# Products of cached keys and sample queries: from VectorE to GpSimd, a page per instruction

## What is computed

```python
q, k, v, u = _project(xs, pos_s, ...)                      # 8 sample rows: RMSNorm, x @ w_in, rotary
k_past = cache_k[l][page_table].reshape(bs, n_past, DIFF_HEADS, 2, QK_DIM)
v_past = cache_v[l][page_table].reshape(bs, n_past, DIFF_HEADS, V_DIM)

def _diff_attn_sample(q, k_new, v_new, k_past, v_past, lam):
    s = jnp.concatenate([_scores(q, k_past), ...], axis=-1)    # einsum over 64 columns, 4 heads x 2 components
    a = _diff_weights(s, lam)                                  # softmax of component 0 minus lam * component 1
    o_past = jnp.einsum('bhqk,bkhd->bqhd', a[..., :n_past], v_past)
    ...
```

## Time and profile before

| | us |
|---|---|
| median of 3 runs | 1735.47 |
| lowest, highest | 1733.54, 1738.26 |
| span of the profiled execution | 1736.7 |
| VectorE busy | 781.7 |
| GpSimd busy | 96.3 |
| 128 key products on VectorE, busy | 157.7 |
| 128 key sums on VectorE, busy | 156.2 |

### The profile page before, as it was taken

How to read it: one execution, slowest core, us unless ns; L and a number is a source line. 1 busy time by engine, 2 the same in 40 slices (tenths; PEclk the granted TensorE clock), 3 DMA queues, 4 the chain that set the end, 5 groups by cost and what they waited for, 6 DMA issues and landing times.

```text
span 1736.7 us, 32091 instructions
## 1 busy us (share of the span) xinstructions
PE 1476.6 (85%) x11950; PEld 593.4 (34%) x11951; DVE 781.7 (45%) x1158; ACT 356.2 (21%) x822; POOL 96.3 (6%) x173
## 2 busy tenths in 40 slices
PE   3868887779788978999999899898899999898870
PEld 2433333346433353333333333232233332232220
DVE  2689879997786335112322232132132132131316
ACT  3212212232222111111211212112112122121220
POOL 0000010000000000000100000000000000000000
PEclk8989995689898857999999999899899999999985
DMA  9557888989898685579999999999999999999976
GB/s 328 179 187 261 279 292 268 335 286 304 297 297 274 241 359 205 226 320 403 428 419 417 418 405 414 401 406 409 395 411 410 403 429 412 395 428 428 426 327 252
DMA packets 127292, 598.10 MB, mean 344 GB/s; under 512 B 20503, under 2 KB 20517, under 8 KB 102026
## 3 DMA queue, kind: packets, MB, share of 16 engines
q1 hardware_dynamic: 109088, 560.20, 81.7%
q10 hardware_dynamic: 8634, 20.00, 3.4%
q0 software_dynamic: 9504, 17.06, 2.6%
HBM read 589.36 MB, written 25.87 MB: 354 GB/s over the span
## 4 chain that ended last, share of the span: by engine, by line
PE 40%; DMA 19%; DVE 2%; issue 1%; ACT 0%; DVEq 0%; SPq 0%; ACTq 0%
PE bank L1511 25%; DMA wts<-in_w_gate_up 19%; PE bank L1548 7%; PE bank L1530 4%; PE bank L1501 1%; PE bank L1618 1%; DVE v_ring L2137 1%; PE bank L1559 1%; PE bank L1599 0%; DVE q_b L2137 0%; DMA h_tok<-h_rows,v_tok 0%; ACT k_T L1155 0%; DVEq L2125 0%; ACT k_T L1138 0%; DVEq L2126 0%
## 5 line engine op out<-in xcount | busy, mean ns | idle before, releaser
L1511 PE MATMUL bank<-wts,h_T 128*32 128x512 f32 x4032 | 447.9, 600 | 17.3 <-DMA wts<-in_w_gate_up 17.3
L2059 DVE TENSOR_SCALAR q_T<-bank 128x512 f32<-128x512 f32 x32 | 22.1, 692 | 640.4 <-PE bank L1511 640.4
L1511 PEld LDWEIGHTS bank<-wts,h_T 128*32 128x32 f32 x4032 | 128.7, 111 | 320.6 <-issue 292.0
L1548 PE MATMUL bank<-wts,k_T 128*32 128x512 f32 x2048 | 229.0, 599 | 7.3 <-issue 4.9
L1530 PE MATMUL bank<-wts,h_T 128*32 128x512 f32 x992 | 129.5, 663 | 47.2 <-DMA wts<-in_w_gate_up 45.4
L1658 DVE TENSOR_TENSOR wts<-wts,q_b 128x1024 f32<-128x1024 f32 x128 | 157.7, 1232 | 23.0 <-DMA wts<-in_cache_k 17.3
L1661 DVE TENSOR_REDUCE sc<-wts 128x16 f32<-128x1024 f32 x128 | 156.2, 1220 | 4.4
L1145 ACT ACTIVATE h_T<-bank 128x512 f32<-128x512 f32 x66 | 35.9, 595 | 576.4 <-PE bank L1501 576.4
L1548 PEld LDWEIGHTS bank<-wts,k_T 128*32 128x32 f32 x2048 | 65.0, 111 | 148.8 <-issue 139.4
L1223 PE MATMUL bank<-wts,h_T 128*8 128x128 f32 (+1 forms) x480 | 93.3, 472 | 11.9 <-ACT h_T L854 6.4
L1155 ACT ACTIVATE k_T<-bank 32x256 f32<-32x256 f32 x256 | 95.7, 374 | 14.2 <-PE bank L1548 10.9
(11 more groups left out here) (328 smaller groups left out, 1372.5 us busy)
## 6 DMA issues: line engine op xcount, KB each, us to landing
wts<-in_w_gate_up SPq DMA_DIRECT2D x126, 2048.0 KB, 18.4
wts<-in_w_down SPq DMA_DIRECT2D x64, 2048.0 KB, 26.6
wts<-in_cache_k SPq DMA_DIRECT2D x256, 256.0 KB, 3.7
v_ring<-in_cache_v SPq DMA_DIRECT2D x160, 256.0 KB, 3.8
wts<-in_cache_v SPq DMA_DIRECT2D x96, 256.0 KB, 3.9
wts<-in_w_in SPq DMA_DIRECT2D x5, 2048.0 KB, 24.1
wts<-y_rows SPq DMA_DIRECT2D x4, 2048.0 KB, 15.6
wts<-in_w_out ACTq DMA_DIRECT2D x8, 512.0 KB, 5.8
```

Source lines behind the costliest of these rows:

```text
L1511: m = nc.tensor.matmul(PS[part][p0:p0 + 32, :], lhs[:, 32 * b:32 * b + 32], rhs[:, part * F + half * 512:part * F + half * 512 + 512], sta ...
L1548: m = nc.tensor.matmul(PS[4][p0:p0 + 32, :], act_T[0][:, k, a0:a0 + 32], chunk[c][:, k, n * 512:(n + 1) * 512], start=(c == 0 and k == 0), ...
```

## The change

Every key product moves to GpSimd. GpSimd now walks through the same schedule; its tap products stand beside heads 4 to 7 and its tables beside the first LayerNorm entries. In its key step it waits for the group's load and multiplies each of the two pages by itself, 128x512, signalling `kprod_done`. VectorE's key step waits for that signal in place of the load and keeps the sum. The switch `KEYS_ON_POOL` is set to all groups. To free semaphores, two sets of them (`xw_loaded`, `y_loaded`) become one (`rows_in`), with a count of 32 in the second use.

```diff
+        PIECE = 512
+        KEYS_ON_POOL = (1, 1)
+        def on_pool(n):
+            return n % KEYS_ON_POOL[1] < KEYS_ON_POOL[0]
+        def first_on_pool(b):
+            return next(g for g in range(NG) if on_pool(b * NG + g))
+        def products_on_pool(n):
+            return sum(on_pool(m) for m in range(n + 1)) * GP * (AW // PIECE)
...
-            k, n = filled(a_full, a_no[("P", TILES)][4])
-            pool.wait_ge(k, n)
...
-            for ct in range(CT):
-                nc.gpsimd.tensor_tensor(tap_w[:, ct, :, :].rearrange("p j (g c) -> p (j g) c", c=32),
...
+            def part_q(j):
+                ct = j - H
+                if 0 <= ct < CT:
+                    if ct == 0:
+                        k, n = filled(a_full, a_no[("P", TILES)][4])
+                        pool.wait_ge(k, n)
...
+                    nc.gpsimd.tensor_tensor(tap_w[:, ct, :, :].rearrange("p j (g c) -> p (j g) c", c=32),
...
+            def part_l(g):
+                if g == 0:
+                    pool.wait_ge(o_full, UNITS)
+                    pool.wait_ge(v_out, 16 * TILES)
...
+            def key_step(b, g):
+                r, n = g % RING, b * NG + g
+                if not on_pool(n):
+                    return
+                if first_on_pool(b) == g:
+                    pool.wait_ge(qb_in, 32 if b == 0 else 16 * (b + 1))
+                pool.wait_ge(k_full[r], 16 * GP * (4 * b + g // RING + 1))
+                for p in range(GP):
+                    for c0 in range(0, AW, PIECE):
+                        cols = slice(c0, c0 + PIECE)
+                        nc.gpsimd.tensor_tensor(k_ring[:, r, p, cols], k_ring[:, r, p, cols],
+                                                q_b[:, b % 2, cols], ALU.mult).then_inc(kprod_done, 1)
...
+            run_with_samples(key_step, value_step, {part: part_q(part[1]) if part[0] == "Q" else
+                                                    part_l(part[1]) if part[0] == "L" else iter(())
+                                                    for part in a_no})
...
-                dve.wait_ge(k_full[r], 16 * GP * (4 * b + g // RING + 1))
-                V.link(mul(k_ring[:, r, :, :], k_ring[:, r, :, :],
-                           q_b[:, b % 2, :].unsqueeze(1).to_broadcast([P, GP, AW])))
+                if on_pool(b * NG + g):
+                    dve.wait_ge(kprod_done, products_on_pool(b * NG + g))
+                else:
+                    dve.wait_ge(k_full[r], 16 * GP * (4 * b + g // RING + 1))
+                    V.link(mul(k_ring[:, r, :, :], k_ring[:, r, :, :],
+                               q_b[:, b % 2, :].unsqueeze(1).to_broadcast([P, GP, AW])))
                 total(sc[:, b % LEAD, GP * g:GP * (g + 1), :],
                       k_ring[:, r, :, :].rearrange("p g (h d) -> p g h d", d=QD)).then_inc(kred_done, 1)
```

More of the change, by code:

```diff
@@ L341, in hybrid_step @@
         v_full = [sem(f"v_full{n}") for n in range(VRING)]
-        xw_loaded = [sem(f"xw_loaded{n}") for n in range(TILES + 1)]
+        rows_in = [sem(f"rows_in{n}") for n in range(TILES + 1)]
         win_in = [sem(f"win_in{n}") for n in range(5)]
@@ L345, in hybrid_step @@
         w_used = [sem(f"w_used{n}") for n in range(6)]
-        y_loaded = [sem(f"y_loaded{n}") for n in range(TILES + 1)]
         last_full = [sem(f"last_full{n}") for n in range(2)]
@@ L698, in _ @@
[L698 to L705, removed]
@@ new lines, in part_l @@
+            def part_l(g):
+                if g == 0:
+                    pool.wait_ge(o_full, UNITS)
+                    pool.wait_ge(v_out, 16 * TILES)
+                    V.link(pool.iota(iota_e[:, :], [[1, E]], base=0, channel_multiplier=0,
+                                     allow_small_or_imprecise_dtypes=True))
+                    V.link(pool.affine_select(out=upper, in_=ones[:, :], compare_op=ALU.is_gt, fill=0.0,
+                                              base=0, pattern=[[1, P]], channel_multiplier=-1))
+                    V.link(pool.iota(row_key, [[-1, E]], base=E - 1, channel_multiplier=0,
+                                     allow_small_or_imprecise_dtypes=True))
+                    V.link(nc.gpsimd.memset(row_key[:, 0:1], FIRST_KEY))
+                    V.link(nc.gpsimd.memset(row_key[:, 1:2], -FIRST_KEY))
+                    V.link(pool.iota(col_key, [[0, 1]], base=E - 1, channel_multiplier=-1,
+                                     allow_small_or_imprecise_dtypes=True))
+                    V.link(nc.gpsimd.memset(col_key[0:1, :], FIRST_KEY))
+                    V.link(pool.affine_select(out=col_key, in_=col_key, compare_op=ALU.not_equal, fill=-FIRST_KEY,
+                                              base=-1, pattern=[[0, 1]], channel_multiplier=1))
+                    yield
+                    V.link(pool.iota(col_e, [[0, 1]], base=0, channel_multiplier=1,
+                                     allow_small_or_imprecise_dtypes=True))
+                    V.link(pool.iota(col_tab, [[1, TCOLS]], base=0, channel_multiplier=0))
+                    V.link(pool.iota(pair_no, [[TOPK * P, TILES + 1], [1, TOPK]], base=1, channel_multiplier=TOPK,
+                                     allow_small_or_imprecise_dtypes=True))
+                    pool.iota(iota_r, [[1, CAP]], base=0, channel_multiplier=0,
+                              allow_small_or_imprecise_dtypes=True).then_inc(ids_done, 1)
+                yield
@@ L1821, in part_w @@
                     if c == 0:
-                        dve.wait_ge(xw_loaded[u], 16)
+                        dve.wait_ge(rows_in[u], 16)
                     if s:
```

36 lines of the change are left out of this document (13 added, 23 removed).

## The result

The changed kernel takes 1740.87 us (median, 1732.23 to 1747.93) against 1735.49 (1730.76 to 1739.77) of the kernel before on the same chip: ratio 1.0031, 95% interval 1.0019 to 1.0043. It is slower by 5 us where 29 faster were forecast. The profiled execution has a span of 1739.0 us. It lies at its median (1740.7 us), the profiled execution of the kernel before lay 2.8 us above its own (1738.3 against 1735.5), so the two traces are only 2.3 us apart in their spans.

A forecast was written before the change was run, and what follows sets the result against it. VectorE was taken to lead up to 390 us, above all in the heads, then TensorE with DMA at 0.90. Stage gains of 11, 4, 2, 9, 2 and 2 make 30 us: 1735.5 - 30 = about 1706 us, range 1680 to 1743.

The forecast's parts named there:

- The price of a page: GpSimd's product over one 512-column page was to take 0.95 us, so 1.9 us for a group of two.
- The estimate from the GPSIMD Engine Reference: Other price for GpSimd's page: 1.12 us, with 4 to 6 us less gain in the heads, some 1711 us.
- rival "slower": In the heads, turns cost more than the products did from 1.3 us a page; 1740 us near 1.3; chance 0.18.
- The first stage: 50 to 118 us: batch 0's maximum ready at about 103, so TensorE's 11.9 us wait for pmax goes; gain 11.
- The ring turns about as fast as before.: Key ring of four slots: VectorE's part falls from 2.4 to 1.2 us, GpSimd's 1.9 comes in; no size given.
- Turns: VectorE instructions with two SBUF inputs wait for GpSimd's pages: some 3 us a prompt tile, 1.35 a head, 8 in LayerNorm.
- Heads and convolution: 265 to 390 us (16 heads of prompt attention) was to gain 9; 390 to 500 (convolution, LayerNorm) 2.
- 118 to 265: Prompt tiles 2 to 4 (118 to 253 us) were to gain 4, the hole made by loads (253 to 265) 2.
- 390 to 555: Convolution and LayerNorm (390 to 500 us) were to gain 2, first routing (500 to 555) 2.
- After 555: Routing without keys, then experts: no further gain, every microsecond won or lost before passes to the end one for one.
- 0.4 of the exponentials: Heads: one key sum no longer covers two exponentials between a head's maximum and its combination; 0.4 us a head, 6 us.
- signs of being wrong: Pages over 1.3 us apart with loads present, VectorE waiting for products rather than turns, or time won by 390 lost by 555.

The follow-up runs named there:

- experiments 3 and 6: 3: GpSimd multiplies constants into a spare tile, VectorE's sums wait for loads alone, 1696.6 us; 6: one GpSimd instruction for a group, 1744.1 us; both on the changed kernel.
- without the copy: Changed kernel with the copy of eight numbers replaced by a sum over one element: 1732.0 us; with pages of 384 columns as well: 1713.4 us.
- 384-column kernel: Changed kernel with each GpSimd page shortened from 512 to its first 384 columns, the others keeping the bare key: 1717.1 us, ratio 0.9902.
- free products: Changed kernel with GpSimd writing 8 columns instead of multiplying a page, so scores are those of bare keys: 1685.5 us, ratio 0.9722.
- split in halves: Changed kernel with GpSimd multiplying each page's first 256 columns, VectorE the others, and the copy as a sum: 1723.8 us, ratio 0.9944.

## Why the prediction was wrong

**The price of a page** is the step that failed. I took 0.95 us from the tap products; the page costs 1.27, 1.22 from start to start. The tap products read broadcast operands and keep 1.91 us for 1024 elements in experiments 3 and 6 too; the pages read plain ones, and two of them cost 2.44. That the kind of operand makes the difference is likely, but no run changes it alone. The prediction saw the difference and put it only into its range. The estimate from the GPSIMD Engine Reference of the Trainium skill, section Elementwise side-by-side cycle accounting, 1.12 us, was the nearer of the two, and also short. It is a quarter of the page's 4497 ns; the 2.1 ns a column and 0.18 us that the runs with 256, 384 and 512 columns give would, as an estimate, make 4.5 us of 2048 columns. So the traces agree with that figure, and what a quarter of it lacks is the fixed part.

How much hangs on the price was rightly sized: the prediction goes from 30 us of gain at 0.95 to a loss of some 5 near 1.3 (its rival "slower"), some 100 us for a microsecond; measured were 69 without the copy and 89 with it. By the prediction's slope a page of 1.00 us gives 1711, and the 384-column kernel has 1717 (1712 to 1724 by its interval). Of the 35 us of the miss 24 come back with the page of 1.00 us, and 19 where the copy is out of the way in both kernels. The other 11 are the last 0.05 us of price and the terms below.

**The first stage**, with its gain of 11, is the term that missed most. GpSimd was to be done with 20 groups at 101 and the maximum at 103. GpSimd is done at 114.8: 11 us are the price (40 pages at 1.22 instead of 0.95), 5 are waits for loads, for which the prediction had nothing, and turns took 5 where 7 were forecast. Then the copy takes the maximum to 124.6. Groups in a burst cost 2.44 us instead of 1.9, and VectorE is idle 23 us in this stage before its sums. Even 11 was too much to hope for: with free products the matmul on pmax stands at 110.4, a gain of 7.5.

**"The ring turns about as fast as before."** From the landing of a group's load to the end of its sum it is 7.8 us in the mean before and 7.4 after; with 384 columns it is 6.1, with free products 4.2. SyncE's waits for sums before it may load the next keys are 87 us before and 90 after, and 68 and 45 with 384 columns and with free products. The sentence was right in its words and wrong in its use: a ring that turns as fast as before lets no load come sooner, so there is little to win.

**The copy** stood in no sum. I had costed what meets a turn in the tiles, the heads and LayerNorm, and left out eight copies of eight numbers, 0.15 us at the median in the trace of before. One of them grew to 8.6 us at the place where TensorE was waiting already; the eight are worth 9 us.

**Turns.** Some 42 us were to come back on VectorE (12 in the tiles, 21.6 in the heads, 8 in LayerNorm); it is 68, 57 without the copies. The heads have 27 of it. There I had three such instructions each; the page's groups show more, line 1806 among them, which has 270 ns more for each head. The direction held: line 1819, for which no row had told, does wait, six of its sixteen instructions for 1.0 to 1.6 us. The Trainium skill's SBUF, section Who interferes with whom, says that a tensor_scalar can contend with GpSimd and a tensor_reduce never does; the trace agrees with both, since line 1819 waits and no sum was ever held. That GpSimd's pages wait in return I had charged only in the first stage.

**Heads and convolution.** The heads were to gain 9, and they lose 3: from the third to the fifth milestone it was 117.1 us, and is 119.8. With free products it is 103.0, so the room was there. 118 to 265 was to gain 6 and gains 4 from the first milestone to the third. 390 to 555 gains 5 (5.9 us late at 387, 1.0 at 558), with 4 forecast.

**After 555** the forecast held in the main: an earlier first gather gives an earlier end. The gather stands at 641.7, 629.4 and 602.7 with the split in halves, 384 columns and free products, 12, 25 and 51 us before that of the earlier trace rows's kernel (653.98), and the spans of the same profiled executions are 15, 27 and 54 us shorter, some 2 us more each time; the changed kernel's span is 2 us longer with the same gather. No run explains these 2 us.

**The rival "slower"** had the mechanism and even the time: at a page near 1.3 us, 1740. Its place was only half right. It said that the first stage would still give most of its 11 us; it lost 7, more than the heads did. Its threshold was miscalculated as well: 2.5 p (60 p + 8) / 120 with the 0.4 of the exponentials exceeds the 2.3 us saved from p = 1.17 on, not from 1.3, so at the pages' 1.22 its own formula has the heads lose 2 to 3 us, as they did. The same 1.3 stands among the signs of being wrong, and pages 1.22 apart did not reach it; another of the signs, VectorE waiting for products rather than for turns, did come. The rival got 0.18 because I took the price near 0.95 for measured, when the rows had it for another form of operand.

What stays open: the share of latency and of turns in the 27 us that only the two together cost, and why one copy was shut out for eight pages while others waited for one. No run separates these further.

## What to carry to other kernels

Before work is moved to a second engine that feeds the first, compare the time of a unit in a burst on the new engine with what it took on the old one: 2.44 us for a group on GpSimd against 2.44 on VectorE left next to nothing to win here, whatever the busy shares said. Dividing every unit between both engines (1.85 us) gained 11 us, where moving all units lost 5, or came out level without the copy, and moving every second one changed nothing. Take the price of an instruction from one with the same kinds of operand, and list every small instruction of the engine that gives turns, even one of 0.15 us, with who waits behind it.

## What was not expected of the hardware

- GpSimd's product in float32, plain operands, 128 partitions: 725 ns for 256 columns, 998 for 384, 1268 for 512, so 2.1 ns a column and some 0.18 us; with both operands broadcast, 256 columns took 653 ns.
- A run of GpSimd pages, starting 1.22 us apart and 1.27 long, shut one of VectorE's eight copies of eight numbers out for 8.6 us. The others that met a run waited for one page at most (0.97 to 1.22 us long), and so did VectorE's products (2.2 us instead of 1.22). With one GpSimd instruction for a group the longest copy was 2.05 us, with a wait between the pages 1.17, with pages of 384 columns 0.36.
- A sum over one element does what the copy does, and took 0.14 us at the longest in all six kernels that have it, five of them with GpSimd at work.
